# Hybrid decoder layer with 32 experts: two expert jobs in a loop body over 18 ring slots, paired down products, transfers of two units

## The reference, cut to what matters

```python
x = x + mix @ w_out                       # after pooling and dilated attention (not touched here)
h2 = rmsnorm(x, norm2_g)                  # 512 tokens x 1024
logits = h2 @ router_w + router_b         # 32 experts
top_v, top_i = lax.top_k(logits, 4)
gates = softmax(top_v)
# for every token and each of its 4 experts e:
gu  = h2 @ w_gate_up[e] + b_gate_up[e]    # 1024 x 2048
act = (clip(up, -7, 7) + 1) * (g * sigmoid(1.702 * g)),  g = minimum(gate, 7)
y   = act @ w_down[e] + b_down[e]         # 1024 x 1024
x   = x + sum over the 4 experts of gate * y
out = rmsnorm(x, final_g)
```

## Time and profile before

| | us or number |
|---|---|
| median of 3 runs | 1361.76 (1358.73 to 1362.21) |
| the profiled execution | 1362.39 |
| its span | 1360.6 |
| PE busy | 1188.6 |
| DVE busy | 502.2 |
| POOL busy | 245.2 |
| ACT busy | 178.5 |
| transfers of weights (line 357) | 384 of 1024 KB |
| jobs (line 1239 x32), chunks (line 1218 x80) | 32, 80 |

### The profile page before, as it was taken

The page is one execution under the profiler, slowest core; times in us unless marked ns, Lnnn a source line. Parts: engine busy times, 40 slices in busy tenths (PEclk is TensorE's granted clock), DMA queues, the critical chain, the costliest instruction groups (busy, mean ns, idle before and its releaser), DMA issues.

```text
span 1360.6 us, 32750 instructions
## 1 busy us (share of the span) xinstructions
PE 1188.6 (87%) x11932; PEld 514.2 (38%) x11933; DVE 502.2 (37%) x1386; ACT 178.5 (13%) x330; POOL 245.2 (18%) x250
## 2 busy tenths in 40 slices
PE   7999999976999989999999998788999898978870
PEld 6744544551343333333333343223333333423220
DVE  2012332343454334444443453333433343433337
ACT  3113332210010101111111100001110010000002
POOL 0063433001112121111111111111112111111110
PEclk9998999977999999999999998889999898988885
DMA  9422120043999999999999999999999999999957
GB/s 379 193 94 77 63 78 1 32 155 142 373 420 419 420 420 419 419 419 419 393 402 381 418 420 420 419 419 419 419 418 417 420 419 420 420 420 420 420 236 308
DMA packets 71453, 454.87 MB, mean 334 GB/s; under 512 B 11013, under 2 KB 11325, under 8 KB 19974
## 3 DMA queue, kind: packets, MB, share of 16 engines
q1 hardware_dynamic: 61374, 430.49, 77.2%
q0 software_dynamic: 9360, 22.08, 4.3%
q10 hardware_dynamic: 696, 1.98, 0.4%
HBM read 444.37 MB, written 14.71 MB: 337 GB/s over the span
## 4 chain that ended last, share of the span: by engine, by line
PE 68%; DMA 24%; issue 3%; DVE 3%; ACT 1%; POOL 0%; SPq 0%; DVEq 0%; POOLq 0%; ACTq 0%
PE bank L649 33%; DMA arena<-in_w_gate_up 20%; PE bank L682 14%; PE bank L433 8%; PE bank L507 4%; DMA arena<-in_w_down 4%; PE bank L451 3%; PE bank L466 1%; DVE xs L1292 1%; PE bank L494 1%; PE bank L480 1%; PE bank L634 1%; PE bank L409 1%; PE bank L588 1%; DMA arena<-y_rows 0%
## 5 line engine op out<-in xcount | busy, mean ns | idle before, releaser
L649 PE MATMUL bank<-arena,hT 128*32 128x512 f32 x5120 | 609.2, 635 | 39.3 <-DMA arena<-in_w_gate_up 30.8
L649 PEld LDWEIGHTS bank<-arena,hT 128*32 128x32 f32 x5120 | 173.0, 116 | 449.3 <-issue 392.7
L682 PE MATMUL bank<-arena,hT 128*32 128x256 f32 x5120 | 288.1, 382 | 14.0 <-DMA arena<-in_w_down 14.0
L682 PEld LDWEIGHTS bank<-arena,hT 128*32 128x32 f32 x5120 | 167.0, 111 | 142.9 <-DMA arena<-in_w_down 22.1
L958 POOL DMA_INDIRECT y_rows<-hT,arena x80 | 80.4, 1005 | 657.3 <-DVE hT L1234 650.0
L1218 DVE TENSOR_TENSOR arena<-bank,gain 128x512 f32<-128x512 f32 x80 | 55.3, 691 | 353.4 <-PE bank L649 353.4
L845 ACT ACT_TABLE_LOAD x48 | 61.6, 1283 | 495.3 <-issue 495.0
L937 POOL DMA_INDIRECT hT<-h_rows,arena x83 | 84.5, 1019 | 200.8 <-issue 195.4
L433 PE MATMUL bank<-hT,arena 128*128 128x512 f32 x224 | 103.8, 612 | 0.0
L845 ACT ACTIVATE arena<-arena 128x256 f32<-128x256 f32 x80 | 33.3, 417 | 412.8 <-DVE arena L1220 412.8
L922 POOL TENSOR_SCALAR arena<-arena,st 128x128 f32<-128x128 f32 (+3 forms) x48 | 51.4, 1082 | 79.5 <-DVE st L1029 79.2
(11 more groups left out here) (138 smaller groups left out, 628.2 us busy)
## 6 DMA issues: line engine op xcount, KB each, us to landing
arena<-in_w_gate_up SPq DMA_DIRECT2D x256, 1024.0 KB, 18.6
arena<-in_w_down SPq DMA_DIRECT2D x128, 1024.0 KB, 19.4
arena<-in_w_in SPq DMA_DIRECT2D x10, 1024.0 KB, 16.7
arena<-y_rows SPq DMA_DIRECT2D x8, 1024.0 KB, 12.3
arena<-in_w_out SPq DMA_DIRECT2D x4, 1024.0 KB, 15.4
arena<-bias_by_dist POOLq DMA_DIRECT2D x6, 512.0 KB, 3.9
xs<-in_x SPq DMA_DIRECT2D x4, 512.0 KB, 8.0
h_rows<-arena POOLq DMA_DIRECT2D x4, 512.0 KB, 2.9
```

What stands on the lines that cost most here:

```text
L649: mm = pe.matmul(bank[c][j * CH:(j + 1) * CH, :].rearrange("p (g n) -> p g n", g=2), xT[:, c, k * CH:(k + 1) * CH], w[:, :, j * Q:(j + 1) ...
L682: mm = pe.matmul(bank[c][j * CH:(j + 1) * CH, 0:Q], aT[:, c, k * CH:(k + 1) * CH], w[:, j * Q:(j + 1) * Q], start=(k == 0), stop=(k == KT ...
```

## The change

1. A job has at most 96 tokens (`JT`, 3 chunks) instead of 128. 32 jobs remain with these inputs if no expert has more than 96 tokens.
2. The loop body holds two jobs. Odd jobs take units 0 to 5 from slots 12 to 17, all other units keep their slots.
3. A transfer carries two units (2 MB), so that a partition's piece is 16 KB and not 8 KB. SP's order for job j+1 in a turn: units 0 to 3 of job j+2, then 6 to 11 of job j+1, then 4 and 5 of job j+2. Before the loop, units 0 to 5 of job 1 are loaded too.
4. PE runs `indices(job + 1)` after the gates of units 0 to 3, not ahead of them, and reads two values per job. The branch on the number of chunks stands at each of the units 0 to 3.
5. The down products of chunks 0 and 1 are made together (`down_pair`): two products of 64 columns with 512 columns of weights per step, into bank 3. They wait for both chunks' activations. Chunk 2 has its own (`down_third`), into bank 4. The gates no longer wait for the bias of the job before.
6. DVE adds the down bias once for the pair; POOL scatters the pair in one transfer with rows of 512 numbers, and starts the third chunk's scatter in every job.
7. At the end PE makes the middle two of the four gate-weighted terms (`gate_diag`, written by ACT, times the rows), DVE adds them in two operations of 512 columns.

```diff
+NCH = 3
+JT = NCH * CH
+EARLY = 4
+HALF = 6
 # SP
+            def ring_slot(half, u):
+                return u + JOB_UNITS if half and u < HALF else u
-                src = w_gate_up[bass.ds(e, 1)].rearrange("e (p k) n -> (e k) p n", p=P)[u]
+                src = w_gate_up[bass.ds(e, 1)].rearrange("e (p m k) n -> (e m) p (k n)", p=P, k=2)[u // 2]
-            sp.dma_start(dst, src).then_inc(unit_full[u], 16)
+            a = ring_slot(half, u)
+            sp.dma_start(ring[:, a:a + 2, :].rearrange("p u n -> p (u n)"), src).then_inc(two_full[u // 2], 16)
+            for n in range(0, HALF, 2):
+                if n == HALF - 2:
+                    sp.wait_ge(ssq_done, 2 * TT)
+                    sp.wait_ge(tr_done, 4 * TT)
+                    for b in range(2):
+                        sp.wait_ge(h2_out[b], 16 * TT // 2)
+                sp.wait_ge(two_full[n // 2], 16)
+                load_two(1, n, 1)
+            ahead, rest, late = range(0, EARLY, 2), range(EARLY, HALF, 2), range(HALF, JOB_UNITS, 2)
+            with sp.Fori(0, more) as pair:
+                for half in range(2):
+                    job = pair * 2 + (1 + half)
+                    e_next = expert(pair * 2 + (2 + half))
+                    load_part(e_next, pair * 2 + (2 + half), half, ahead, pair * 2 + half)
+                    load_part(expert(job), job, 1 - half, late, pair * 2 + half, counted(job))
+                    load_part(e_next, pair * 2 + (2 + half), half, rest, pair * 2 + half)
 # PE
+                def down_pair(k):
+                    w = unit(KT + k // 2)[:, (k % 2) * D:(k % 2 + 1) * D]
+                    for g in range(2):
+                        mm = pe.matmul(bank[3][g * 2 * CH:(g + 1) * 2 * CH, :],
+                                       aT_pair[:, k].rearrange("p c s -> p (c s)"), w[:, g * 2 * Q:(g + 1) * 2 * Q],
+                                       start=(k == 0), stop=(k == KT - 1), tile_position=(0, g * 2 * CH))
-                indices(job + 1)
                 pe.wait_ge(x_done, job + 1)
+                for k in range(KT // 2):
+                    if k % 2 == 0:
+                        pe.wait_ge(two_full[k // 2], full)
+                    with pe.If(chunks > 2):
+                        gate_step(2, k)
+                    gate_step(1, k)
+                    gate_step(0, k)
+                indices(job + 1)
                 ...
+                pe.wait_ge(act_done, low + AHEAD)
+                for k in range(KT):
+                    down_pair(k)
+            with pe.Fori(0, pairs) as pair:
+                for half in range(2):
+                    run_job(pair * 2 + half, half, ...)
 # POOL
+                pool.wait_ge(y_done, job + 2)
+                pool.indirect_dma_start(y_rows, ... idx_s[:, 0:1] ..., yb_third, ...)
+                pool.indirect_dma_start(y_halves, ... idx_s[:, 1:2] ..., yb_pair, ...)
 # DVE, end
-                for k in range(TOPK):
+                for k in (0, TOPK - 1):
+                dve.wait_ge(mid_sum, t + 1)
+                for n in range(2):
+                    ins = dve.tensor_tensor(part, bank[2 * (t % 2) + n][:, :], part, ALU.add)
```

More of the change, by code:

```diff
@@ L363, in load_job, with load_part @@
+            def load_part(e, job, half, units, free_of, low=None):
+                for u in units:
+                    wait_read(free_of, u, low)
                     sp.sem_inc(waited_sp, 1)
-                    sp.wait_ge(unit_full[u], job * 16)
+                    sp.wait_ge(two_full[u // 2], job * 16)
                     sp.sem_inc(waited_sp, 1)
[L366 to L380, removed]
@@ L631, in indices @@
                 pe.wait_ge(hot_done, job + 1)
-                for c in range(NCH):
+                for c in range(LISTS):
                     for t in range(TT):
@@ L641, in _, with run_job, unit @@
             pe.wait_ge(jobs_done, 2)
-            def run_job(job, chunks, before_job, low):
+            def run_job(job, half, chunks, low):
+                full = job * 16 + 16
+                def unit(u):
+                    return ring[:, u + JOB_UNITS if half and u < HALF else u, :]
                 def gate_step(c, k):
-                    w = ring[:, k, :].rearrange("p (g n) -> p g n", g=2)
+                    w = unit(k).rearrange("p (g n) -> p g n", g=2)
                     for j in range(4):
@@ L655, in gate_step @@
                         mm.then_inc(units_used, 1)
[L657 to L664, removed]
                 def gate_rest(c):
                     for k in range(KT // 2, KT):
-                        if c > 0:
-                            pe.wait_ge(unit_full[k], job * 16 + 16)
+                        if c > 0 and k % 2 == 0:
+                            pe.wait_ge(two_full[k // 2], full)
@@ L690, in run_job @@
-                every = range(KT)
+                    if k % 2 == 1 and k < KT - 1:
+                        mm.then_inc(units_used, 1)
+                pe.wait_ge(x_done, job + 1)
+                for k in range(KT // 2):
+                    if k % 2 == 0:
+                        pe.wait_ge(two_full[k // 2], full)
+                    with pe.If(chunks > 2):
+                        gate_step(2, k)
+                    gate_step(1, k)
+                    gate_step(0, k)
                 indices(job + 1)
-                pe.wait_ge(x_done, job + 1)
@@ new lines, in _ @@
+            with pe.Fori(0, pairs) as pair:
+                for half in range(2):
+                    job = pair * 2 + half
+                    run_job(job, half,
+                            pe.value_load(jobs_i[0:1, 2, bass.ds(job, 1)], min_val=LEAST, max_val=NCH),
+                            pe.value_load(jobs_i[0:1, 3, bass.ds(job + 1, 1)], min_val=4, max_val=COUNT_MAX))
+            for t in range(TT):
+                pe.wait_ge(diag_done, t + 1)
+                if t >= 2:
+                    pe.wait_ge(mid_read, t - 1)
+                    pe.wait_ge(sum_done, t - 1)
+                for k in (1, 2):
+                    pe.wait_ge(y_in[t][k // 2], 16)
+                    for n in range(2):
+                        c = (k % 2) * D + n * 512
+                        mm = pe.matmul(bank[2 * (t % 2) + n][:, :], gate_diag[:, t, k - 1],
+                                       ring[:, 3 * t + k // 2, c:c + 512], start=(k == 1), stop=(k == 2))
+                mm.then_inc(mid_sum, 1)
@@ L861, in _ @@
             act.dma_start(final_gain, final_g.partition_broadcast(P)).then_inc(gain_in, 16)
+            act.wait_ge(gates_done, 1)
+            for t in range(TT):
+                for k in (1, 2):
+                    ins = act.activation(gate_diag[:, t, k - 1], ident, ACT.Copy,
+                                         scale=gates[:, TOPK * t + k:TOPK * t + k + 1])
+                ins.then_inc(diag_done, 1)
             for t in range(TT):
@@ L1243, in _ @@
                 with dve.If(chunks > 2):
-                    with dve.If(chunks > 3):
-                        swiglu(3)
                     swiglu(2)
```

262 lines of the change are left out of this document (134 added, 128 removed).

## The result

| | us |
|---|---|
| kernel before, median of 4 | 1360.61 (1358.73 to 1362.21) |
| changed kernel, median of 4 | 1345.22 (1344.82 to 1346.18) |
| ratio | 0.9891, 95% interval 0.9879 to 0.9904 |
| profiled execution of the changed kernel | 1345.49, span 1343.5 |

The forecast was 1341, in a range of 1329 to 1365. The change makes the kernel 15 us faster.

The account below looks back on a forecast made before the run. The prediction took the weights' transfers to bound the kernel from 326 us on, with PE setting where slots come free. It summed 1362.4 - 13 - 6 - 1 - 1.5 = 1340.9 us, predicting 1341, range 1329 to 1365.

Parts of the forecast that it names:

- Parts 1 and 2: Six units of job 1 loaded ahead of the loop, and paired downs: PE ends at 1308.1, not 1321.1, -13.0 us.
- The order at the end: End of the loop: the transfers behind job 30's units 6 and 7 are 12 units, so these land at 1265.0.
- Early units: Idle queues up to 320 us: six units of job 1 fit in, 15.8 us of work.
- The stalls of 5.7 + 1.6 us: Early in the loop: SP waits 5.7 us for slots 6 and 7, then 1.6 us for the next pair.
- Rival D: SP's fixed load order stops at PE's slots, early units bring no lead: the 13 us go, 1354 us, chance 0.09.
- The gap and the pair: PE's gap between jobs hidden, 31.8 us per 3-chunk job; pair downs 6.9 us, waiting 3.1 in 2-chunk jobs.
- Rivals B and C: PE's gap and slow clock: B, gap partly hidden, 1356 us, chance 0.20; C, full gap, 1372, up to 1379, 0.14.
- Part 3: Weight transfers of two units, 16 KB packets instead of 8 KB: half of the fit's 12.8 us taken, -6 us.
- Rival A: Weight transfers gain all that the two queues' fit allows, 13 to 18 us: 1329 to 1334 us, chance 0.15.
- Part 4: Start: job 0's gates no longer stand behind the indices; between 0 and -3 us, taken as -1.
- Part 5: Final sums behind PE's last downs: -1.7 us, and +0.2 for the pair's wider bias add, together -1.5 us.
- The signs that I had listed: 3-chunk jobs every 31.5-32 us, no dip at 640-740, pair 6.9 us, PE's end 1301, q1's time per MB 0.7% lower.

Follow-up runs that it names:

- x5_tail: Changed kernel, with units 6 to 11 of job 30 loaded ahead of units 0 to 3 of job 31 in the last turn: 1336.16 us, ratio 0.9825.
- x10_one_tail: Changed kernel with 1 MB transfers and the last pair of jobs loaded in the order of use: 1352.44 us, ratio 0.9946 to the kernel before.
- x3_no_early: Changed kernel, SyncE waiting for the job list and TensorE's use of job 0's first unit before loading job 1's units 0 to 5: 1347.03 us, ratio 0.9909.
- x4_dve_sums: Changed kernel with all four gate-weighted end terms on VectorE, no end products on TensorE: 1347.45 us, ratio 0.9902 to the kernel before.
- x7_one_early0: Changed kernel with 1 MB transfers and no unit of job j+1 loaded ahead of job j's, in the whole loop: 1365.40 us, ratio 1.0025.

## Why the time was right and its reasons were not

By the steps of the prediction:

1. **Parts 1 and 2, -13.0 us: wrong.** With 1 MB transfers Parts 1, 2, 4 and 5 together gave 0.4 us, by the profiles 3.2 up to PE's end (1317.95 against 1321.15). Most of the miss is one step: "the transfers behind units 6 and 7 of job 30 are 12 units: these land at 1296.5 - 31.5 = 1265.0". The queue itself was on time. In the run with 1 MB, 11.50 MB of weights were left at 1265.0 us, 11.0 units where I had 12. But the landing came at 1273.65, 8.65 us late. From that landing on, the weights' queue moved this much in that run (to 1320 us):

```profile
q1 hardware_dynamic: 1135, 8.21, 44.5%
```

   That is 7.8 units, although 12 had still to land: 4.2 were under way in pieces. In the kernel before it is this, from the same landing at 1276.05 to 1322:

```profile
q1 hardware_dynamic: 1930, 13.99, 73.2%
```

   13.3 units of 16, so 2.7 under way. The reason is in the semaphore events of the traces. Each transfer leaves sixteen reports, as many as there are DMA engines, and has landed with the last. For units 6 and 7 of job 30 in the changed kernel, ten reports came from 1248.18 to 1248.97, the fourteenth at 1256.50, the last two at 1260.25 and 1260.74. The last is 9.6 us behind the mean of the sixteen, 4.1 MB at 425 GB/s; and 8.47 of the 12.58 MB behind it were moved after it, which leaves 4.1 MB moved ahead. In the kernel before the last report of unit 7 is 6.5 us behind the mean, 2.7 MB, against 2.8 MB by the same count.

   This spread builds up while the queue never stops. In the kernel before, the reports of unit 5 lie within 0.6 us at job 0 and 6.2 at job 10, within 0.3 at job 13, behind the dip from 640 to 740 us, and within 10.3 at job 30. In the changed kernel those of units 6 and 7 lie within 0.5 us at job 0 and 13.7 at job 20, and then stay between 11.8 and 12.9 up to job 30. So the landing is later behind the same bytes in a kernel that has no dip. The Trainium skill ("DMA: Bandwidth & Descriptors", Latency and other measured facts) says that two of the sixteen engines are usually slower than the rest. The trace agrees in part: two reports come 3.8 and 4.2 us behind the fourteenth, but that one is itself 8.3 us behind the first, and the reports do not say which engine sent them. The stretch from this landing to PE's end was forecast as 43.1 us and took 44.3.
2. **The order at the end: in the sum, but not seen as a cost.** I counted twelve units behind that landing and took the order as given. Four others, units 0 to 3 of job 31, stood in front of it before anybody needed them. Put behind, they were worth some 7 us twice (x5_tail, x10_one_tail).
3. **Early units, "15.8 us of work fit": wrong cause.** The row shows the work done early, but slots limit the lead, and x3_no_early reaches the same lead less 3.2 us from 320 us on. Without the head start some 2 us are lost. What is left of Parts 1 and 2 is the six slots and the shorter job: either of them may be what removes the dip at 640 to 740, and no run has one without the other, so their shares stay open. The stalls of 5.7 + 1.6 us came as forecast (7.9). Rival D, that the lead is lost to SP's order, is wrong in its place (no dip repeats in the loop) and right in one thing: the order does take lead back, at the last turn.
4. **The gap and the pair: right.** 31.83 us for 31.8, 7.09 for 6.9, a wait of 3.01 ahead of line 731 for 3.1, 8.78 us with the slow clock for 6.9 + 1.7. Here is a 2-chunk job's pair:

```profile
1041.91 7.94 PE L703 MATMUL bank<-arena,hT 128*32 128x512 f32 x48 [7.11 <-DMA arena<-in_w_gate_up]
1052.86 7.50 PE L731 MATMUL bank<-arena,hT 128*64 128x512 f32 x26 [3.01 <-DVE hT L1297]
```

   Rivals B and C fall with the 31.83 us. The wait costs nothing in the loop: PE had waited 7.11 us for weights just before.
5. **Part 3, -6 us: mis-sized.** It is 14.4 us. The fit of the two queues gave 8.4 ns a packet and 12.8 us; the runs gave 12.4. I halved a number that the rows had given, out of distrust of two unlike queues; the fit was low, not high. The figure of the Trainium skill ("DMA: Bandwidth & Descriptors", Why small descriptors are slow), 3 cycles a packet, led to an estimate of 0.6%; the rate changed by 1.6%, so here the measurement decides against it. Rival A had the transfers right (13 to 18 us), but its sum of 1329 to 1334 rests on the same -13 and is 11 to 16 us too low.
6. **Part 4, -1 us:** the gates of job 0 start at 316.37, not 320.34, 4.0 us earlier and beyond my bound of 3. But the same code ahead of the loop gave 312.66 in another run, so how much of the 4.0 is the change's is not known, and what it is worth at the end was not tried.
7. **Part 5, -1.5 us: in line, but not clear of noise.** Behind PE's end the profiles have 0.9 us less than before and 2.0 less than x4_dve_sums; that run's ratio gives 1.5, with 0 in its interval.

So the terms -13, -1 and -1.5 were together -0.4, and the -6 was -14.4: errors of 15 and 8 us of opposite sign, which left 1341 against 1345 (the execution that the sum started from was also 1.8 us over its median). That the number came out was luck. The signs that I had listed (31.8 us jobs, no dip at 640, the pair's 7 us) all came and did not show it; only PE's end, 1304.9 for 1301, and the queue's time per MB, 2.3% lower for 0.7%, pointed there.

## What to carry to other kernels

A forecast of a stream's end is not one of a landing: leave the units that are under way between them, more of them where the queue has not stopped for long, and count what stands in the queue ahead of the one that matters. Where a queue never idles, the length of each partition's run in a transfer is paid in full; where another engine is the bound for a stretch it is not, so try such an edit together with the one that frees the queue. In the last turn of a loop that loads ahead, put the loads back in the order of use.

## What was not expected of the hardware

- A row of a partition costs its engine some 14 ns beside its bytes (12.4 per packet of the list), the same from 16 to 8 KB and from 8 to 4 KB: 425, 417 and 406 GB/s.
- With 18 slots some 4.4 MB of the queue had been moved ahead of the unit that landed (4.2 units); with 12 slots it was 2.8 MB. The sixteen reports of one transfer drift apart to 12 or 13 us over hundreds of us without a stop, and a stop brings them together again.
- With equal packets of 8 KB the kernels with 18 slots move 417 to 418 GB/s where the kernel before moves 419 to 420, with 16 KB 425 against 426. The order of the loads is not the cause (x7_one_early0). From 740 to 1000 us the weights alone are the same, 104.32 MB with 18 slots and 1 MB transfers and 104.39 before, and the software queue moved less, 4.01 against 4.57 MB; from 450 to 640 us it is the weights that are 0.9% less. What the cause is stays open.
- Two kernels with the same work ahead of the loop differed by 3.7 us at the loop's start (312.66 and 316.37), and by bytes the one that started early (x5_tail) was still ahead at 1200 us, by 1.9 MB or 4.5 us. Its timed runs also spread over 8 us, those of the changed kernel over 1.4; why was not looked into.
